# b_down added as the expert's column in the copy of yT, zeros in DRAM, late modulation in f16 halves

## The reference, cut to what matters

```python
mod = (silu(c) @ w_ada + b_ada).reshape(B, 6, 1, D)      # six rows of 1024

def expert_block(args):                                  # 64 rows a block in the kernel
    xblk, e = args
    gu = xblk @ w_gu[e] + b_gu[e]
    gate = minimum(gu[:, ::2], 7); up = clip(gu[:, 1::2], -7, 7)
    act = (up + 1) * gate * sigmoid(1.702 * gate)
    return act @ w_down[e] + b_down[e]

y = yb.reshape(-1, D)[dest] * gate_sorted[:, None]
return zeros_like(h).at[tok_sorted].add(y)
```

## Time and profile before

| | |
|---|---|
| time, median of 3 runs | 2680.45 us (2677.73 to 2681.34) |
| the profiled execution: its time, its span | 2680.32 us, 2678.6 us |
| TensorE busy | 2439.7 us, 91% |
| VectorE busy | 1797.7 us, 67% |
| ScalarE busy | 1553.6 us, 58% |
| GpSimd busy | 799.2 us, 30% |
| mean granted TensorE clock | 0.967 |
| HBM read, written | 496.99 MB, 38.92 MB |

### The profile page before, as it was taken

How to read it: one execution, slowest core, us unless ns; L and a number is a source line. 1 busy time by engine, 2 the same in 40 slices (tenths; PEclk the granted TensorE clock), 3 DMA queues, 4 the chain that set the end, 5 groups by cost and what they waited for, 6 DMA issues and landing times. The chain is left out here.

```text
span 2678.6 us, 135745 instructions
## 1 busy us (share of the span) xinstructions
PE 2439.7 (91%) x57165; PEld 2162.2 (81%) x57165; DVE 1797.7 (67%) x2118; ACT 1553.6 (58%) x1964; POOL 799.2 (30%) x629
## 2 busy tenths in 40 slices
PE   6999998999989758999999999888998999999993
PEld 2555558999985448999898989888898999999993
DVE  3784986666657773361818386778777786789883
ACT  4523544555554442462827476777776676778773
POOL 3111105677740121221122222323222223232321
PEclk8899998999999968999999999999999999999996
DMA  8621001011023274381929496889888887899966
GB/s 286 248 76 56 1 1 49 25 31 31 23 70 101 95 291 138 119 308 29 356 73 331 125 370 225 305 312 376 320 304 310 311 299 256 281 337 359 344 238 207
DMA packets 123432, 536.90 MB, mean 200 GB/s; under 512 B 12237, under 2 KB 12609, under 8 KB 90561
## 3 DMA queue, kind: packets, MB, share of 16 engines
q1 hardware_dynamic: 107120, 481.80, 47.9%
q0 software_dynamic: 14880, 48.91, 8.2%
q10 hardware_dynamic: 1360, 5.24, 0.5%
HBM read 496.99 MB, written 38.92 MB: 200 GB/s over the span
## 5 line engine op out<-in xcount | busy, mean ns | idle before, releaser
L2499 PE MATMUL ps<-qkv,weights 128*128 128x64 f16 x10496 | 937.8, 193 | 65.9 <-DVE weights L1915 32.9
L2499 PEld LDWEIGHTS ps<-qkv,weights 128*128 128x128 f16 x10496 | 921.9, 98 | 82.4 <-issue 41.4
L2501 PE MATMUL ps<-qkv,weights 128*128 128x64 f16 x10496 | 937.4, 193 | 2.3 <-issue 2.3
L2500 PE MATMUL ps<-qkv,weights 128*128 128x64 f16 x10496 | 937.3, 193 | 0.5 <-issue 0.5
L2501 PEld LDWEIGHTS ps<-qkv,weights 128*128 128x128 f16 x10496 | 922.4, 98 | 0.6 <-issue 0.6
L2500 PEld LDWEIGHTS ps<-qkv,weights 128*128 128x128 f16 x10496 | 922.4, 98 | 0.0
L1915 DVE SCALAR_TENSOR_TENSOR weights<-hT,weights 128x2048 f16<-128x2048 f16 (+1 forms) x256 | 585.9, 2338 | 167.4 <-ACT weights L1299 137.4
L1299 ACT ACTIVATE weights<-hT 128x2048 f16 (+1 forms) x256 | 527.8, 2103 | 83.9 <-DMA hT<-in_w_gu_dram 67.0
L2516 PE MATMUL ps<-qkv,weights 128*128 128x64 f16 x5248 | 472.1, 193 | 23.4 <-DVE weights L1920 21.1
L2516 PEld LDWEIGHTS ps<-qkv,weights 128*128 128x128 f16 x5248 | 461.3, 98 | 30.8 <-DVE weights L1920 26.3
L2517 PE MATMUL ps<-qkv,weights 128*128 128x64 f16 x5248 | 471.8, 193 | 0.0
(11 more groups left out here) (446 smaller groups left out, 4305.0 us busy)
## 6 DMA issues: line engine op xcount, KB each, us to landing
hT<-in_w_gu_dram SPq DMA_DIRECT2D x256, 1024.0 KB, 9.1
qkv<-in_w_down_dram SPq DMA_DIRECT2D x128, 1024.0 KB, 6.1
weights<-in_w_ada_dram SPq DMA_DIRECT2D x8, 2048.0 KB, 14.1
qkv<-in_w_in_dram SPq DMA_DIRECT2D x4, 2048.0 KB, 9.2
qkv<-in_w_ada_dram SPq DMA_DIRECT2D x4, 2048.0 KB, 9.3
hT<-decay_rows SPq DMA_DIRECT2D x20, 256.0 KB, 3.3
hT<-beta_rows SPq DMA_DIRECT2D x20, 256.0 KB, 3.3
qkv<-in_x_dram ACTq DMA_DIRECT2D x4, 1024.0 KB, 8.1
```

The source lines that it names most:

```text
L2499: pe.matmul(dst, ghi[k][:, b, c], xT[:, 0, k, :], start=first, stop=False, skip_group_check=True)
L2500: pe.matmul(dst, ghi[k][:, b, c], xT[:, 1, k, :], start=False, stop=False, skip_group_check=True)
L2501: last = pe.matmul(dst, glo[k][:, b, c], xT[:, 0, k, :], start=False, stop=end, skip_group_check=True)
```

## The change

- The gate-weighted start of y is gone: lgm, mixe3, gT3, bd3, y_start, copy_y_start, store_y_start and what waits for them. b_down is loaded once, 32 x 1024; TensorE turns it with eight transposes (behind the small matmuls of the block tables), ScalarE copies it after the token one-hots into bdT, 128 partitions x (32 experts x 8 columns), in the memory of the ones and iota.
- y_d starts as zeros in DRAM: SyncE stores the zero region slot(5) over it with two DMAs of 2 MB, between the row loads of the context steps and the latent loop; the wait before the loop counts them as well.
- The copy of yT goes from ScalarE to VectorE: one scalar_tensor_tensor, yT = PSUM x scale + bdT column of the block's expert (whose number is loaded into a register). In VectorE's loop it stands after the gate halves of block t+2 and before the down halves of block t+1. It waits for all four down chunks of block t and for turn_y.
- Late modulation: the sums are scaled by 64 (csw); ScalarE copies a high f16 half of each, at z groups 0 (four), 3, 5, 6 and 7; GpSimd subtracts it for the low half; TensorE adds up both with 64 f16 matmuls against a column of 1/64. ScalarE's copy of brows (at m = 1) waits for these matmuls.

```diff
+        bdT = sb("ones_and_iota_then_b_down", [P, NE * KD])
+        ones, iota = bdT[:, 0:P], bdT[:, P:2 * P]
         tri = sb("tri", [P, DIRS, P])
...
+        csw = sb("csw", [P, KD])
         scA = sb("scA", [P, 2, KD])
@@ -615,7 +610,10 @@
             sp.dma_start(h2_d[SEQ:, :], zero[0:B, :].bitcast(F16)).then_inc(s_zero, 16)
             for s in range(1, NC):
                 load_rows(s, False)
-            sp.wait_ge(s_zero, 33)
+            for i in range(2):
+                sp.dma_start(y_d[i * SEQ // 2:(i + 1) * SEQ // 2, :].rearrange("(p r) d -> p (r d)", p=P),
+                             slot(5)).then_inc(s_zero, 16)
+            sp.wait_ge(s_zero, 65)
             with sp.Fori(NC, NA) as s:
                 load_rows(s, True)
 
...
-            for j in range(3):
-                sp.dma_start(bdn[j * NE:(j + 1) * NE, :], b_down[0]).then_inc(s_small, 16)
+            sp.dma_start(bdn, b_down[0]).then_inc(s_small, 16)
...
-            sp.wait_ge(s_bd, NT)
+            sp.wait_ge(s_bdT, 1)
...
+            link(pool.memset(ones16, 1.0 / WSCALE))
@@ -790,6 +788,11 @@
                 link(pool.tensor_scalar(lrs[:], mv[:, :, 1], EPS, None, ALU.add))
                 pool.tensor_tensor(lrs[:], lrs[:], mhalf[:, 0:H], ALU.pow).then_inc(s_lrs, 1)
 
+
+            for q in range(FIRST, NADA):
+                pool.wait_ge(s_adar, q + 1)
+                high, low = (sum_halves[q - FIRST][:, j] for j in range(2))
+                pool.tensor_tensor(low, sums_of[q - FIRST], high, ALU.subtract).then_inc(s_colT, 1)
...
             pool.sem_inc(s_al, 1)
             gather(0)
-            for n in range(NT):
-                store_y_start(n)
             gather(1)
             gather(2)
             low_act(0)
             gather(3)
             low_act(1)
-            for i in range(2):
-                pool.wait_ge(s_yin[i], 16 * (5 - 2 * i))
             with pool.Fori(1, MAXB) as t:
                 with pool.If(t <= nprev):
                     gather(t + 3)
@@ -1090,6 +1085,14 @@
             for g in range(G_Z, G_QKV):
                 take(g)
                 act.activation(zs[:, g - G_Z, :], ps[:, g % 6, :], ACT.Silu, scale=1.0 / WSCALE).then_inc(s_pjf, 1)
+                for q in {0: range(FIRST, FIRST + 4), 3: (8,), 5: (9,), 6: (10,), 7: (11,)}.get(g - G_Z, ()):
+                    act.wait_ge(s_mod, q + 1)
+                    if q == FIRST:
+                        act.wait_ge(s_hl, NA)
+                        act.wait_ge(s_adaT, FIRST)
+                    if q >= FIRST + 4:
+                        act.wait_ge(s_colT, q - 3)
+                    act.activation(sum_halves[q - FIRST][:, 0], sums_of[q - FIRST], ACT.Copy).then_inc(s_adar, 1)
                 if g == G_Z + 4:
                     high_w(4)
 
...
+                    act.wait_ge(s_adaT, FIRST + 1)
@@ -1334,12 +1333,6 @@
                 act.wait_ge(s_a, t + 1)
                 reached(act, s_dn, t, DK, DK)
                 act.activation(ah, act_n, ACT.Copy).then_inc(s_ah, 1)
-
-            def copy_yT(t):
-                act.wait_ge(s_dn, t * DK + 2 * DK)
-                reached(act, s_ty, t, 1, EMPTY)
-                act.activation(yT, ps[:, BT, :].rearrange("p (c t) -> p c t", c=8), ACT.Copy,
-                               scale=1.0 / (ALPHA * WSCALE * WSCALE)).then_inc(s_yT, 1)
 
             def scale_y(t):
                 act.wait_ge(s_ty, t + (EMPTY + 1))
...
-            for n in range(4):
-                copy_y_start(n)
-            token_one_hots(0)
-            token_one_hots(1)
-            copy_y_start(4)
-            token_one_hots(2)
-            token_one_hots(3)
-            for k in range(3):
+            for q in range(4):
+                token_one_hots(q)
+            act.wait_ge(s_bdT, 1)
+            act.activation(bdT[:].rearrange("p (e c) -> p c e", e=NE), ps[:, 2, 0:NE * KD].rearrange("p (c e) -> p c e", c=KD),
+                           ACT.Copy).then_inc(s_bdT, 1)
+            for k in range(4):
                 high_gate_up(0, 0, k)
-            copy_y_start(5)
-            high_gate_up(0, 0, 3)
-            copy_y_start(6)
             copy_xT(0)
             name_rows(1)
-            high_gate_up(0, 0, 4)
-            copy_y_start(7)
-            for k in range(5, GK):
@@ -1408,7 +1386,6 @@
             next_gate_up(2, new2 > 0, r2, LAST)
             next_down(1, new > 0, r)
             high_act(1)
-            copy_yT(0)
             with act.Fori(1, MAXB) as t:
                 with act.If(t <= nprev):
                     new1, new2, r1, r2 = flags_and_ranks(t)
@@ -1422,11 +1399,9 @@
                     next_gate_up(t + 2, new2 > 0, r2, range(5, GK))
                     next_down(t + 1, new1 > new2, r1)
                     high_act(t + 1)
-                    copy_yT(t)
                     scale_y(t - 1)
                     next_down(t + 1, new1 + new2 > 1, r1)
             scale_y(nprev)
-            copy_yT(nlast)
             scale_y(nlast)
 
             act.wait_ge(s_g2, 1)
@@ -1496,14 +1471,15 @@
                 if q == 7:
                     dve.wait_ge(s_hl, NA - 1)
                 sums = sums_of[q - FIRST]
-                link(dve.tensor_scalar(sums, staged(q)[:, 0, :], cs[:, 0, 0:1], None, ALU.mult))
+                link(dve.tensor_scalar(sums, staged(q)[:, 0, :], csw[:, 0:1], None, ALU.mult))
                 for k in range(1, KD):
-                    link(dve.scalar_tensor_tensor(sums, staged(q)[:, k, :], cs[:, k, 0:1], sums, ALU.mult, ALU.add))
+                    link(dve.scalar_tensor_tensor(sums, staged(q)[:, k, :], csw[:, k:k + 1], sums, ALU.mult, ALU.add))
                 dve.sem_inc(s_mod, 1)
 
             for i in range(4):
                 norm_x(i)
             mod_columns(0)
+            link(dve.tensor_scalar(csw[:], cs[:, :, 0], WSCALE, None, ALU.mult))
             dve.wait_ge(s_modA, 1)
             dve.scalar_tensor_tensor(wbal, wba[:], WSCALE, wbah, ALU.mult, ALU.subtract).then_inc(s_modA, 1)
@@ -1756,7 +1732,6 @@
                 link(dve.tensor_tensor(lg, ps[:, 1, 0:NE], rb, ALU.add))
                 dve.sem_inc(s_lg, 1)
                 link(dve.max(top[:, n, :], lg))
-                dve.tensor_scalar(lgm[:, n, :], lg, top[:, n, 0:1], None, ALU.subtract)
                 link(dve.max_index(top_i[:], top[:, n, :], lg))
                 link(dve.tensor_copy(top_f[:], top_i[:]))
@@ -1953,6 +1920,13 @@
                 dve.tensor_tensor(gate_up_n, both, bias[:, bass.ds(e * 16, 16)].unsqueeze(2).to_broadcast([P, 16, B]),
                                   ALU.add).then_inc(s_gr, 1)
 
+            def copy_yT(t, e):
+                dve.wait_ge(s_dn, t * DK + 2 * DK)
+                reached(dve, s_ty, t, 1, EMPTY)
+                dve.scalar_tensor_tensor(yT, ps[:, BT, :].rearrange("p (c t) -> p c t", c=8), 1.0 / (ALPHA * WSCALE * WSCALE),
+                                         bdT[:, bass.ds(e * 8, 8)].unsqueeze(2).to_broadcast([P, 8, B]), ALU.mult,
+                                         ALU.add).then_inc(s_yT, 1)
+
             def swiglu(t):
                 chain.turn(t)
                 dve.wait_ge(s_gr, t + 2)
...
+            dve.wait_ge(s_bdT, 2)
             nprev = dve.value_load(meta[0:1, N_AT:N_AT + 1], min_val=MINB - 2, max_val=MAXB - 2)
             nlast = nprev + 1
...
             new, r = flag(1), rank_before(1)
             next_gate_up(1, new > 0, r, range(4), 4)
-            for i in range(2):
-                dve.wait_ge(s_yin[i], 16 * (5 - 2 * i))
             read_gate_up(0, expert(0))
             swiglu(0)
             next_gate_up(1, new > 0, r, LAST, 4)
@@ -1989,6 +1963,7 @@
             swiglu(1)
             next_gate_up(2, new2 > 0, r2, LAST, 4)
             next_down(1, new, r)
+            copy_yT(0, expert(0))
             with dve.Fori(1, MAXB) as t:
                 with dve.If(t <= nprev):
                     code = dve.value_load(code_of[0:1, bass.ds(t, 1)], min_val=0, max_val=256 * NE - 1)
@@ -1998,8 +1973,10 @@
                     read_gate_up(t + 1, e)
                     swiglu(t + 1)
                     next_gate_up(t + 2, new2 > 0, r2, range(4, GK))
+                    copy_yT(t, expert(t))
                     next_down(t + 1, new1, r1)
                     dve.sem_inc(s_idle, 1)
+            copy_yT(nlast, expert(nlast))
@@ -2172,11 +2149,13 @@
                 if m == 1:
                     pe.wait_ge(s_mod, NADA)
                     pe.wait_ge(s_sgf, NT)
+                    pe.wait_ge(s_colT, NADA)
                     for q in range(FIRST, NADA):
                         for a in range(4):
                             n = 4 * (q - FIRST) + a
-                            last = pe.matmul(ps[:, 6, n:n + 1], sums_of[q - FIRST][:, a * P:(a + 1) * P], ones[:, 0:1],
-                                             start=True, stop=True)
+                            for j in range(2):
+                                last = pe.matmul(ps[:, 6, n:n + 1], sum_halves[q - FIRST][:, j, a * P:(a + 1) * P],
```

(38 more changed lines are left out.)

38 lines of the change are left out of this document (5 added, 33 removed).

## The result

| | median us | runs | ratio to before, 95% |
|---|---|---|---|
| before | 2676.97 (2664.28 to 2685.81) | 18 | |
| after | 2688.34 (2682.16 to 2697.95) | 18 | 1.0044 [1.0032, 1.0055] |

The account below looks back on a forecast made before the run. TensorE, 91% busy, was taken to bound the kernel, other engines counting only where it waits. Terms -8.2 + 0 - 0.9 - 13.2 + 24 - 3 + 0.1 = -1.2 gave 2679.1 us, range 2665 to 2693.

Parts of the forecast that it names:

- Late modulation: Front end: 64 f16 matmuls replace 32 one-column f32 ones on TensorE's gapless list, -8.2 us; no clock gain counted.
- Zeros: Two 2 MB DMAs between context steps and latent loop, hidden where SyncE has nothing to move: 0, bounds 0 to +3.
- Router: Gate and bias work in the middle: eight VectorE subtractions and small operations removed from the router, -0.9 us.
- Start: Start of the experts: stores and their waits go, block 1's first matmul comes sooner, -13.2 us, bounds -18 to -8.
- (c): Nine two-block loop cycles where VectorE's copy waits for the whole down ahead of low down halves: +2.9 each, taken +24.
- (b): Double places, two new experts in a row, nine times: ScalarE's wait shrinks, copy mostly hidden: -0.3 each, together -3.
- the pieces of eight: Eight gate halves run in one piece on VectorE in double places: copy costs 0 to 0.7, less ScalarE's 0.5.
- The rival: Slower: copy not hidden in the double places, costing 1.1 instead of -0.3 each, +13 in all, 2692 us; chance 0.27.
- (a): Loop blocks with no low down halves behind the copy, or none needed soon: 0, as VectorE idles there.

Follow-up runs that it names:

- e3: The kernel before with only the late modulation in f16 halves: median 2667.09 us, ratio 0.9956 to before.
- e4: The kernel before with 223 idle semaphore increments ahead of TensorE's first wait: median 2712.53 us, ratio 1.0117 to before.
- e1: The changed kernel with 33 idle semaphore increments ahead of TensorE's first wait, putting its loop back in its old place: 2686.04 us, ratio 1.0028 to before.
- e7: The changed kernel with 161 idle increments ahead of TensorE's first wait: median 2696.10 us, ratio 1.0083 to before.
- e11: The changed kernel with 20 idle increments ahead of TensorE's first wait: 2689.37 us, one run.
- e12: The changed kernel with 100 idle increments ahead of TensorE's first wait: 2689.69 us, one run.
- e6: e1 with the yT copy back on ScalarE at its old place and b_down left out of the result: 2661.31 us, ratio 0.9938 to before.
- e10: The kernel before with the second expert's loads held until TensorE's first chunk of block 1 is done: 2670.62 us, ratio 0.9972 to before.
- e5: e1 with the yT copy placed by case, ahead of the down halves or between the second and third: 2670.21 us, ratio 0.9968 to before.
- e9: e5 with the second expert's loads held until TensorE's first chunk of block 1 is done: 2662.58 us, ratio 0.9948 to before.

## Why the prediction was wrong

- **Late modulation**: right in its mechanism, -10.4 for -8.2. The term I left out ("I don't count a gain from it") is the 2.1 us of projections at half clock behind the slow matmuls. Matmul pace and spare time of the halves came out as worked out.
- **Zeros**: right, 0. **Router**: -0.7 for -0.9, and the nearness is luck: e3, with the router of before, has -0.5 over the same stretch, so the missing subtractions are worth 0.2 at most. What gives e3 its 0.5 is open.
- **Start**: mechanism right (stores, their wait and DMA time go, the rows of block 1 come sooner), size wrong: -8.1 for -13.2. The step that failed is "VectorE's last low half ...; TensorE's last chunk 1.6 later": VectorE waited 6.6 for it, by 5.2 us of pauses in TensorE's first pass, which wait for instructions. Before, a pause of 2.3 us of this kind already stood inside block 0 and the sum had no term for it. The one at the return was kept, as forecast (5.3 for 6.3). The size is rough: in e3 and e4, with the code of before in this stretch, it took 2.7 and 3.4 us longer than in before, and against them the change gives 11.
- **(c), the nine cycles**: right. The cycle shown above lost 2.3 where I had 2.9, less some waits. Blocks 53 to 81 take +24.4 in the profiled run; over the four kernels with the copy at this place and the short pause (e1, e7, e11, e12: mean 561.6) against the four with it on ScalarE (before, e3, e6, e10: 538.9) it is +22.8, for +24.
- **(b), the double places**: wrong in sign. By the same means blocks 2 to 53 take 1032.6 against 1028.1: +4.5 for -3. By block, the first of a pair gains 1.0 us, the second loses 1.2, and the one ahead of both loses 0.3. e1's timeline shows why. In the first block of a pair the gain is there: low down waits 0.37 us for ScalarE instead of 1.44. But in the second block the copy stands ahead of the down halves with nothing to run behind:

```profile
1300.08 0.69 DVE L1926 SCALAR_TENSOR_TENSOR qkv<-ps,nes_and_iota_then_b_down 128x512 f32<-128x512 f32 x1
1301.13 8.90 DVE L1887 SCALAR_TENSOR_TENSOR weights<-qkv,weights 128x2048 f16<-128x2048 f32 x4 [0.37 <-ACT weights L1304]
...
1314.33 0.69 DVE L1926 SCALAR_TENSOR_TENSOR qkv<-ps,nes_and_iota_then_b_down 128x512 f32<-128x512 f32 x1 [1.32 <-issue]
1314.96 2.29 DVE L1887 SCALAR_TENSOR_TENSOR weights<-qkv,weights 128x2048 f16<-128x2048 f32 x1
1318.81 2.29 DVE L1887 SCALAR_TENSOR_TENSOR weights<-qkv,weights 128x2048 f16<-128x2048 f32 x1 [1.57 <-ACT weights L1304]
...
1326.60 1.23 DVE L1920 TENSOR_TENSOR qkv<-ps,same 128x1024 f32<-128x1024 f32 x1 [0.41 <-issue]
```

  The copy starts 1.32 us of issue after the swiglu, which I read as its register load and the branch; the second half then waits 1.57 for ScalarE, itself 1.95 behind a load (0.81 before); read to read this block takes 16.7 us and took 15.0. My sum had priced the pieces of eight and the first block of the pair and never the second one. The rival named the double places and overstated them, +1.1 for each of nine where it is +0.5.
- **(a), the free blocks**: wrong, "0". VectorE does idle there, as I said; the loss is on TensorE, of which the step says nothing. It is 0.24 us each at the loop's return, which no part of the change asks for: TensorE's list is 33 instructions shorter, and the place of the loop costs. Over the loop it is 1602.0 against the mean of 1594.3 for the four other places, some 8 us; single traces of one and the same loop differ by 6, so the size is rough, but e4 shows the same 8.6 against before.

Beyond these, the DeltaNet dips took 3.4 us off this one profiled run. Failed steps in order of size: (a) +8, (b) +7.5, start +5. Together that is 20 us; that the time came out only 9 above the forecast is owed in part to luck, these dips and the 2.1 us of clock that the sum had left out.

## What to carry to other kernels

An instruction that reads what another engine finishes late belongs behind the work that doesn't need it, and where its cover changes with the case, no fixed place tried here was right in both: choosing it by branches gave back 16 us here. Price a moved instruction in every kind of iteration, the ones with nothing before it above all. Before believing a small loss in a long loop, look at the return of the loop: a few instructions more or fewer ahead of it moved this one by 0.24 us a turn.

## What the runs showed of the hardware that I had not expected

- The return of TensorE's loop took 0.66 us from the start of the last matmul to that of the first in three kernels (at +0 and +256 instructions ahead of it), and 0.42 at +20, +33, +34, +100 and +161, with no packet of the instruction queue in either case.
- During 10 us of one-column f32 matmuls the granted clock fell to 0.50 of 2.4 GHz, which is the 1.2 level, and it stayed there for some 4 us of full projections, at a price of 2.1 us; with f16 matmuls in their place it didn't fall.
- TensorE's first pass through a long loop has pauses of 2 to 5 us, each of which ends 1.3 to 2.6 us behind a 16 KB packet of the instruction queue. They were 10.5 us in all with the weight loads beside them (e5) and 6.5 with the loads held back (e9).
